# Where the weight quarters of the up projections stand in on-chip memory, and the order in which they are made, in a two-block transformer kernel

## The reference, cut to what matters

```python
def conv_glu_ffn(h, w_up, w_conv, b_conv, w_down):      # first block
    a, u = jnp.split(h @ w_up, 2, axis=-1)               # h: 512x1024, w_up: 1024x5632
    return (jax.nn.gelu(dwconv3(a, w_conv, b_conv)) * u) @ w_down
...
def conv_ffn(xn, w_up, conv_w, w_down):                  # second block, twice
    up = xn @ w_up
    a, g = jnp.split(up, 2, axis=-1)
    a = causal_dwconv(a, conv_w)
    return (jax.nn.silu(a) * g) @ w_down
```

## Time and profile before

| | |
|---|---|
| median of 3 runs | 2075.5 us (2075.18 to 2075.77) |
| profiled execution, its own time | 2075.54 us |
| its span, first to last instruction | 2073.8 us |
| granted TensorE clock, mean | 1.00 of full speed |
| TensorE matmuls busy | 2063.9 us (100%) |
| GpSimd busy | 1307.5 us (63%) |
| VectorE busy | 1178.4 us (57%) |
| ScalarE busy | 889.6 us (43%) |

### The profile page before, as it was taken

How to read it: one execution, slowest core, us unless ns; L and a number is a source line. 1 busy time by engine, 2 the same in 40 slices (tenths; PEclk the granted TensorE clock), 3 DMA queues, 4 the chain that set the end, 5 groups by cost and what they waited for, 6 DMA issues and landing times.

```text
span 2073.8 us, 31464 instructions
## 1 busy us (share of the span) xinstructions
PE 2063.9 (100%) x10848; PEld 1736.9 (84%) x10848; DVE 1178.4 (57%) x2027; ACT 889.6 (43%) x1544; POOL 1307.5 (63%) x1716
## 2 busy tenths in 40 slices
PE   9999999999999999999999999999999999999999
PEld 7788888888899888888888898888777778989887
DVE  6567574334677882233457777413477757687800
ACT  5544465323534353332253344324466655334421
POOL 8553346556587876645457888655554537787853
PEclk9999999999999999999999999999999999999999
DMA  6333222323323233233233333333322222333332
GB/s 234 118 106 114 63 67 83 96 82 122 92 82 109 95 107 111 88 94 101 89 93 98 96 103 107 104 104 102 102 82 82 82 62 82 105 99 102 105 105 75
DMA packets 62716, 204.34 MB, mean 99 GB/s; under 512 B 7056, under 2 KB 8720, under 8 KB 62576
## 3 DMA queue, kind: packets, MB, share of 16 engines
q1 hardware_dynamic: 60624, 201.54, 31.5%
q10 hardware_dynamic: 1952, 0.99, 0.2%
HBM read 199.42 MB, written 2.26 MB: 97 GB/s over the span
## 4 chain that ended last, share of the span: by engine, by line
PE 90%; DVE 6%; DVEq 1%; ACT 1%; issue 1%; DMA 0%; ACTq 0%; SPq 0%
PE bank L1989 21%; PE bank L1990 21%; PE bank L1991 21%; PE bank L2305 4%; PE bank L2304 4%; PE bank L2303 4%; DVE FL L1673 2%; PE bank L2398 1%; PE bank L2424 1%; PE bank L2410 1%; PE bank L2371 1%; PE bank L2373 1%; PE bank L2372 1%; PE bank L2455 1%; PE bank L2043 1%
## 5 line engine op out<-in xcount | busy, mean ns | idle before, releaser
L552 POOL TENSOR_TENSOR WL<-RAW,WH 128x256 fp32r<-128x256 f32 x992 | 778.2, 818 | 594.2 <-ACT WH L734 588.8
L586 POOL TENSOR_TENSOR WL<-RAW,WH 128x256 fp32r<-128x256 f32 x594 | 470.2, 827 | 106.4 <-ACT WH L989 104.5
L1989 PE MATMUL bank<-XH,WH 128*128 128x512 f32 x1256 | 493.6, 393 | 1.4 <-DVE bank L1666 0.6
L1990 PE MATMUL bank<-XL,WH 128*128 128x512 f32 x1256 | 489.3, 390 | 0.0
L1991 PE MATMUL bank<-XH,WL 128*128 128x512 f32 x1256 | 489.1, 389 | 0.0
L734 ACT ACTIVATE WH<-RAW 128x1024 fp32r<-128x1024 f32 (+1 forms) x258 | 258.8, 1011 | 221.5 <-PE bank L1991 194.6
L989 ACT ACTIVATE WH<-RAW 128x512 fp32r<-128x512 f32 x297 | 173.3, 625 | 314.9 <-PE bank L2305 137.3
L1989 PEld LDWEIGHTS bank<-XH,WH 128*128 128x128 f32 x1256 | 235.8, 188 | 53.5 <-issue 2.8
L1991 PEld LDWEIGHTS bank<-XH,WL 128*128 128x128 f32 x1256 | 235.8, 188 | 49.7
L1990 PEld LDWEIGHTS bank<-XL,WH 128*128 128x128 f32 x1256 | 236.0, 188 | 46.7
L1989 PE MATMUL bank<-FH,WH 128*128 128x512 f32 x528 | 206.1, 390 | 0.6 <-DVE FL L1673 0.5
(11 more groups left out here) (388 smaller groups left out, 3667.5 us busy)
## 6 DMA issues: line engine op xcount, KB each, us to landing
RAW<-in_w_up SPq DMA_DIRECT2D x132, 512.0 KB, 3.5
RAW<-in_w_att SPq DMA_DIRECT2D x50, 512.0 KB, 3.5
RAW<-in_w_down SPq DMA_DIRECT2D x48, 448.0 KB, 3.3
RAW<-in_w_down SPq DMA_DIRECT2D x24, 512.0 KB, 3.5
RAW<-in_w_ain SPq DMA_DIRECT2D x24, 512.0 KB, 3.5
RAW<-in_w_fa SPq DMA_DIRECT2D x24, 512.0 KB, 3.5
RAW<-in_w_mrg SPq DMA_DIRECT2D x15, 512.0 KB, 4.1
RAW<-in_w_mrg SPq DMA_DIRECT2D x24, 256.0 KB, 2.7
```

The lines of the kernel that those rows point to most:

```text
L552: last = nc.gpsimd.tensor_tensor(WL[:, s, w], RAW[:, s, w], WH[:, s, w].bitcast(F32), ALU.subtract)
L586: last = nc.gpsimd.tensor_tensor(WL[:, s, w], RAW[:, s_raw, r], WH[:, s, w].bitcast(F32), ALU.subtract)
L1989: mm(dst[:, 0:width], WH[:, s, w], a, start=start and k == 0, stop=False)
L1990: mm(dst[:, 0:width], WH[:, s, w], b, start=False, stop=False)
```

## The change

The four slots' halves become eight places. The quarters of pairs 4 to 21 are numbered in TensorE's order of reading (`POS`, with `SKIP` added so that the last one ends at the end of the fourth slot), and quarter number p stands in place p mod 8. A quarter may be made when the one eight numbers before it has been read (`used_before`); for the first ones of a stage that is a count of whole units. `RAW` keeps its old layout. Each engine makes the quarters pair by pair: of a pair W in the order 22, 11, 12, s1, s2, s4, s3, of a plain pair p0 to p3. TensorE waits for each quarter by itself, in plain pairs too (`pair`), and counts each one as read (`w_used`, or `unit_done` for those that end a unit).

```diff
+KINDS = "PPPPWPWPWPWPWPWPWPWPWP"
+PARTS = {"P": ("p0", "p1", "p2", "p3"), "W": ("11", "12", "s1", "22", "s2", "s4", "s3")}
+MAKE = {"P": ("p0", "p1", "p2", "p3"), "W": ("22", "11", "12", "s1", "s2", "s4", "s3")}
+ENDS = {"p1": 1, "s4": 1, "p3": 2, "s3": 2}
...
+for _m in range(PAIR0, FB):
+    for _q in PARTS[KINDS[_m]]:
+        POS[_m, _q] = len(POS)
...
+SKIP = -len(POS) % (2 * NSLOT)
+POS = {_k: _p + SKIP for _k, _p in POS.items()}
...
+    def used_before(l, m, q):
+
+        p = POS[m, q] - 2 * NSLOT
+        while p >= 0 and p not in AT_POS:
+            p -= 2 * NSLOT
+        if p < 0:
+            return unit_done, U[f"up{l}"] + 2 * PAIR0 + p // 2 + 1
+        return used(l, *AT_POS[p])
+
+    def tile_at(l, m, q):
+
+        p = POS[m, q]
+        return (U[f"up{l}"] + p // 2) % NSLOT, p % 2
...
@@ GpSimd
+            for m in range(PAIR0, FB):
+                for q in MAKE[KINDS[m]]:
+                    low_quarter(l, m, q)
...
@@ ScalarE
+            early = 0
+            for x in range(PAIR0 - 1, FB - 1):
+                m = x + 1
+                make = MAKE[KINDS[m]]
+                for q in make[0:3] if KINDS[m] == "W" else make[0:2]:
+                    hi_quarter(m, q)
+                if KINDS[x - 1] == "W":
+                    part(x - 1)
+                if KINDS[x] == "W":
+                    first_copy(x)
+                for q in make[3:5] if KINDS[m] == "W" else make[2:4]:
+                    hi_quarter(m, q)
+                for q in make[5:7]:
+                    hi_quarter(m, q)
+                if KINDS[x] == "P":
+                    part(x)
+                    if x >= FB - 1 - 2 * EARLY_F and early < EARLY_F:
+                        f_high(early)
+                        early += 1
...
@@ VectorE
-            for i in range(NWINO):
-                w = NWINO * l + i
-                m = PAIR0 + 2 * i
-                if i:
-                    pair_second(m - 2)
-                weight_sums(w)
-                if i:
-                    glu(m - 2)
-                first_out(m - 1)
-                second_out(m - 1)
-                if NWINO - EARLY_F <= i < NWINO:
-                    f_low(i - (NWINO - EARLY_F))
-                pair_first(w, m)
+            early = 0
+            for x in range(PAIR0 - 1, FB - 1):
+                if KINDS[x - 1] == "W":
+                    pair_second(x - 1)
+                if KINDS[x + 1] == "W":
+                    weight_sums(x + 1)
+                if KINDS[x - 1] == "W":
+                    glu(x - 1)
+                if KINDS[x] == "W":
+                    pair_first(x)
+                    continue
+                first_out(x)
+                second_out(x)
+                if x >= FB + 1 - 2 * EARLY_F and early < EARLY_F:
+                    f_low(early)
+                    early += 1
             m = FB - 2
             pair_second(m)
             glu(m)
-            for n in range(EARLY_F, 9):
+            for n in range(early, 9):
                 f_low(n)
             first_out(m + 1)
...
@@ TensorE
+        def pair(name, l, m):
+
+            for j in range(2):
+                pe.wait_ge(lin_free, O[name] + 2 * m + j + 1)
...
+                    pe.wait_ge(*made(w_lo, lo_ready, l, m, q))
...
+                    last.then_inc(used(l, m, q)[0], 1)
```

More of the change, by code:

```diff
@@ L186 @@
 PAIR0 = 4
-NWINO = 9
+KINDS = "PPPPWPWPWPWPWPWPWPWPWP"
+NWINO = KINDS.count("W")
 HM = S // 2
@@ L586, in low_quarter @@
                 last = nc.gpsimd.tensor_tensor(WL[:, s, w], RAW[:, s_raw, r], WH[:, s, w].bitcast(F32), ALU.subtract)
-            return last
+            last.then_inc(made(w_lo, lo_ready, l, m, q)[0], 1)
         def up_lows(name, l):
@@ L1046, in up @@
+            while early < EARLY_F:
+                f_high(early)
+                early += 1
             m = FB - 2
+            part(m)
             act.wait_ge(unit_done, u0 + 2 * m + 2)
-            hi_quarter(s3, 1, s3, 1).then_inc(hi_ready, 1)
-            part(m)
             whole(u0 + 2 * m + 4)
@@ L1703, in up, with weight_sums @@
             second_out(2)
[L1705 to L1711, removed]
+            def weight_sums(m):
+                w = wino_index(l, m)
+                a11, a12, a21, a22 = (quarter(RAW, *raw_at(l, m, q)) for q in ("11", "12", "s3", "22"))
+                dve.wait_ge(*made(w_lo, lo_ready, l, m, "22"))
                 v.tensor_tensor(a22, a21, a22, ALU.add).then_inc(w_sum, 1)
[L1713 removed]
+                dve.wait_ge(*made(w_lo, lo_ready, l, m, "11"))
                 dve.drain()
@@ L1968, in _, with unit @@
         mm = nc.tensor.matmul
-        def unit(u0, j, i, per, kc, xh, xl, k0, dst, start=True, stop=True, width=S, ready=None, halfway=None,
-                 second_low=False):
+        def unit(u0, j, i, per, kc, xh, xl, k0, dst, start=True, stop=True, width=S, ready=None, halfway=None):
             s = (u0 + j) % NSLOT
-            if not second_low:
-                pe.wait_ge(lo_ready, i * per + (u0 + j + 1))
+            pe.wait_ge(lo_ready, i * per + (u0 + j + 1))
             for k in range(kc):
-                if second_low and k == kc // 2:
-                    pe.wait_ge(lo_ready, u0 + j + 1)
                 if halfway and k == kc // 2:
@@ new lines, in pair @@
+        def pair(name, l, m):
+            for j in range(2):
+                pe.wait_ge(lin_free, O[name] + 2 * m + j + 1)
+                bank_ = LB[(O[name] + j) % 2]
+                for h in range(2):
+                    q = PARTS["P"][2 * j + h]
+                    s, half = tile_at(l, m, q)
+                    pe.wait_ge(*made(w_lo, lo_ready, l, m, q))
+                    for k in range(HK):
+                        c = slice(half * UW // 2 + k * P, half * UW // 2 + (k + 1) * P)
+                        kk = HK * h + k
+                        mm(bank_[:], WH[:, s, c], XH[:, kk, :], start=kk == 0, stop=False)
+                        mm(bank_[:], WH[:, s, c], XL[:, kk, :], start=False, stop=False)
+                        last = mm(bank_[:], WL[:, s, c], XH[:, kk, :], start=False, stop=kk == KB - 1)
+                    last.then_inc(used(l, m, q)[0], 1)
@@ L2301, in product, with wino @@
+        def wino(name, l, m):
+            o = O[name] + 2 * m
+            def product(n, q, xh, xl):
+                s, h = tile_at(l, m, q)
+                pe.wait_ge(*made(w_lo, lo_ready, l, m, q))
                 for k in range(HK):
                     c = slice(h * UW // 2 + k * P, h * UW // 2 + (k + 1) * P)
-                    mm(dst, WH[:, s, c], xh[:, k, :], start=k == 0, stop=False)
-                    mm(dst, WH[:, s, c], xl[:, k, :], start=False, stop=False)
-                    last = mm(dst, WL[:, s, c], xh[:, k, :], start=False, stop=k == HK - 1)
@@ new lines, in product @@
+                    last = mm(WP[n], WL[:, s, c], xh[:, k, :], start=False, stop=k == HK - 1)
+                last.then_inc(used(l, m, q)[0], 1)
+            follows = KINDS[m - 1] == "W"
+            pe.wait_ge(lin_free, o + 1 if follows else o)
+            product(1, "11", XH[:, 0:HK, 0:HM], XL[:, 0:HK, 0:HM])
+            product(2, "12", XH[:, HK:KB, 0:HM], XL[:, HK:KB, 0:HM])
+            if "W" not in KINDS[:m]:
+                pe.wait_ge(xd_lo, 4 * l + 4)
+            if follows:
+                pe.wait_ge(lin_free, o + 2)
```

167 lines of the change are left out of this document (52 added, 115 removed).

## The result

| | before | changed |
|---|---|---|
| median | 2075.64 us (2075.18 to 2076.13, 8 runs) | 2082.03 us (2081.91 to 2082.92, 8 runs) |
| span of the profiled execution | 2073.8 us | 2080.3 us |

The ratio is 1.0031, 95% interval 1.002 to 1.0042: 6.4 us slower. 2083.1 us was forecast.

The account below looks back on a forecast made before the run. TensorE was taken to bound the kernel, with no gap in the up stages. Entry and exit costs, 3 × (1.55 + 0.97) = 7.6 us on 2075.54, gave 2083.1 us; eight in ten from 2079.8 to 2088.0.

Parts of the forecast that it names:

- Bound and rounds: Up stages: TensorE bounds the kernel without any gap, and the change costs 0 us in the rounds.
- the 4.5 us of margin: Rounds of `up0`: smallest time between a quarter being ready and TensorE wanting it, 4.5 us, so new waits cost nothing.
- Into the rounds: First pair W of each stage: quarter 12 waits for all of unit 7, delaying the copy and s4; 1.55 us a stage.
- two stops, of 1 us and of 0.5 us: First pair W: TensorE waits about 1 us ahead of the second product, about 0.5 us ahead of the sixth.
- Out of the rounds: End of each up stage: one f_low more in VectorE's chain that TensorE waits for, 0.97 us a stage.
- The bound of 0.6 us from below: Lower bound on the extra f_low's cost, if the loads free some time on VectorE ahead: 0.6 us.
- the prediction's 0.6 us: Down stage's last block: time TensorE already loses before the change waiting for VectorE's last low, 0.6 us.
- Only the exit: Rival, 8%: quarter 12 is ready in time after all, leaving only the extra low's cost; 2078.4 us.
- only the entry: Rival, 8%: VectorE makes up the extra low out of its waits in the last round; 2080.2 us.
- A new wait in each round: Rival, 9%: copy or plain pair's lows come too late in later rounds, 10 us on top; 2093 us.
- Counting by signals: Rival, 4%: 108 more read signals cost TensorE time, 1.1 us (2084.2), or 2.8 us by the skill's rule (2085.9).
- Not slower: Rival, 5%: small entry gaps and a hidden extra low, if the first lows end by 764.2; 2075.5 or 2073.9 us.

Follow-up runs that it names:

- spread_gaps: Changed kernel with SKIP = 0 and the five numbers skipped one by one ahead of pairs 8, 10, 12, 14 and 16: 2076.74 us.
- copy_first: Changed kernel with the copy of the first product ahead of roundings p0 and p1 in ScalarE's order: 2081.19 us.
- late_high: half_six, with ScalarE waiting before rounding the down stage's fourth unit until VectorE has made seventeen of the 22 lows: 2073.27 us.
- four_lows: Changed kernel with four f_low in the rounds and five in the first group behind pair 20: 2083.58 us, one run.
- six_lows: Changed kernel with six f_low in the rounds again, three in the first group behind pair 20: 2080.64 us.
- half_signal: Changed kernel with one signal more: quarter 12 of pair 4 waits only for the first half of unit 7: 2076.71 us.
- half_six: Changed kernel with both edits: the signal for half of unit 7, and six f_low in the rounds: 2075.60 us.

## Why the prediction was right, point by point

**Bound and rounds.** TensorE's starts show no gap in any later round of any stage, as forecast, so the 4.5 us of margin were enough. spread_gaps took a quarter of lookahead away at five points of each stage, and there is still none. How much of the margin is left there was not measured.

**Into the rounds.** Right in place, cause and chain; the term of 1.55 us a stage measured 1.66, 1.60 and 1.96. The steps of `up0`: rounding of 12 at T + 0.20 (0.26 foreseen), the low's start at T + 0.91 (0.97), the fourth sum at T + 2.43 (2.4), `first_out(3)` at T + 3.49 (3.37), `part(3)` at T + 6.77 (6.66), s4 at T + 8.77 (8.64, and 0.10 for the restart). What the prediction had wrong is the weight of the steps. It put only the first gap inside the sum, made the rest the copy's, and looked for two stops, of 1 us and of 0.5 us. There are three. The second, at s1, was not foreseen: the low of s1 comes right behind that of 12 in GpSimd's queue while VectorE's sum runs beside it. Of the 1.66 us, the first gap and its restart take 1.05 and the second 0.47, so only 0.16 was left to the copy: copy_first got back 0.16, 0.09 and 0.44 us. Each gap ahead of the copy only takes away from what TensorE has to wait for it, and so the sum came near although a gap was missing in it: the last link of the chain was worked out from T.

The third stage's 0.3 us more are VectorE's: between two instructions of `first_out(3)`'s convolution it stood for 0.43 us with nothing to wait for that the profile shows. The rows in the changed kernel's timeline, and the second of them in the timeline of the kernel before:

```profile
1770.29 0.75 DVE L1328 SCALAR_TENSOR_TENSOR TC<-bank,PAR,TC 128x510 f32<-128x510 f32 x1
1771.47 0.75 DVE L1328 SCALAR_TENSOR_TENSOR TC<-bank,PAR,TC 128x511 f32<-128x511 f32 x1 [0.43 <-issue]
```

```profile
1760.93 0.75 DVE L1317 SCALAR_TENSOR_TENSOR TC<-bank,PAR,TC 128x511 f32<-128x511 f32 x1 [0.43 <-issue]
```

So the change did not bring this stop. It stands at the same instruction of the third stage in the kernel before and in every run here; before, TensorE never stood behind it, and the change put it into the chain that TensorE waits for. The prediction took the rows of `up0` for all three stages and could not see it. Why VectorE stood is open. copy_first fits with it: the stop is still in its trace, but the third stage's extra was in the third gap, and went.

**Out of the rounds.** Right in place and cause, too large in size: 0.97 us foreseen, 0.43 to 0.47 measured. The step that was mis-sized is the cost of one `f_low`, taken from means of groups. A low has two prices here. In late_high, where GpSimd is still or gives way, eight take 4.91 us, 0.61 each. Beside GpSimd's lows they take 1.15 each, as the growth of the first group shows. How many lows of VectorE meet one of GpSimd's depends on GpSimd's work in that stretch, which the change leaves nearly where it was. So one more low in the first group pays the high price, 1.15 us, and fewer of the second group do, which gives back 0.70. What is left is 0.45 us, and 0.57 in four_lows, both below the low's own 0.61; the rest of the difference is open. four_lows and late_high show the two prices from two sides. The bound of 0.6 us from below, given for another reason, was itself too high. And the loss that was there before is larger than the prediction's 0.6 us, which leaves out what follows the stop at the last block: against the 14.96 us of late_high the first pass of `up0` lost 0.82 us before and 1.26 after, where 1.5 was foreseen.

**Rivals.** Only the exit and only the entry: six_lows and half_signal show that both are there, with 1.4 and 5.3 us, and half_six that they add up. A new wait in each round: none. Counting by signals: half_six, with over a hundred signals more, is within 0.1 us of the kernel before. So neither the 1.1 us is seen nor the 2.8 us that the prediction worked out, as an estimate, from the Trainium skill ("TensorE: Matmul & The Clock Gate", The cost: per-tile semaphore tail), whose figure is for the matmuls of tiles packed into the array. Not slower: the first group of lows ended at 766.96, not by 764.2, and the 1.54 us by which the down stage starts later do not make up for that.

The forecast was 2083.1 us and 2082.03 came: +0.6 us from entries that cost more than foreseen, −1.6 from exits that cost less. The two errors partly cancel, and that much of the nearness is luck.

## What to carry to other kernels

Where the bounding engine has no gap in a stage, a new order of buffers can at most keep that, so look at its edges: what the first items of a ring have to wait for when the ring before it is released in coarser steps, and where the last number has to fall. Here one quarter of a stage's 99 had its place too late, and a signal for half a unit gave back 5.3 us. Next, look at what else an edit moves along: a loop limit that shifted by one round put an instruction from free time into the chain that the next stage waits for. A stop that has always been in the trace without cost can come into such a chain too. And if a chain of VectorE instructions with two inputs in on-chip memory sets an end, see what GpSimd does beside it, and whether that could come later.

## What the runs showed of the hardware

VectorE's and GpSimd's instructions with two inputs in SBUF take turns. The median `f_low` (128x512) took 868 ns, the shortest 678 and the longest 1232 in the changed kernel:

```profile
L1684 DVE TENSOR_TENSOR FL<-FR,FH x66: 678/868/1232, 666.7 to 1970.0; 128x512 fp32r<-128x512 f32 x66
```

In late_high the median is 692 ns. Started one after the other they come 0.61 us apart when GpSimd is still, and 1.15 us apart when a low of GpSimd (128x256, two of them 1.42 us in the rows at the entry of the kernel before) stands between each two. 0.61 + 0.71 is 1.3, so one waits for the other in all but 0.2 us. An instruction of VectorE with one input in PSUM is not slowed: `first_out(3)`'s first row at 581.18 takes 0.69 us beside GpSimd's lows, where the sum before it, with both inputs in SBUF, takes 1.14. The Trainium skill ("SBUF — State Buffer", SBUF: two separate sides) says so: the two engines share a pair of ports, and an instruction of GpSimd and one of VectorE with two SBUF inputs shut each other out for their whole length. The trace agrees but for the 0.2 us. It does not show strict turns: in late_high two lows of VectorE passed in a row while GpSimd's first stood.

The other surprise is that one line for ScalarE, which makes it wait, is worth 2.2 us in the kernel before and 2.3 us in half_six. A first matmul behind a stop adds 0.07 to 0.11 us of its own to the stop, at columns of 256 and of 512: the distance to the next start is 0.19 or 0.22 in place of 0.12, and 0.34 in place of 0.23.
